# A two-layer encoder trunk on one core: first tiles and memory keys fetched a stage ahead, two units paired at a seam, roots and low parts moved

## What is computed

```python
def even_layer(x, mem, ...):              # layer 0
    h = rmsnorm(x, norm_g)
    qa, ka, va, ga, qb, kb, vb, gb, qm, gm = split_cols(h @ w_in, EVEN_SPLITS)
    oa = sliding_window_sink_attention(qa, ka, va, sinks)     # 8 heads
    ob = stick_breaking_attention(qb, kb, vb)                 # 8 heads
    om = memory_attention(qm, rmsnorm(mem, mem_norm_g), w_mem_kv)   # 4 heads, 256 memory tokens
    y = concatenate([oa * silu(ga), ob * silu(gb), om * silu(gm)])
    return x + y @ w_out                                      # y: 1280 columns

def odd_layer(x, mem, ...):               # layer 1
    h = rmsnorm(x, norm_g)
    qc, ckv, qi, ki, wi, gc, qm, gm = split_cols(h @ w_in, ODD_SPLITS)
    ckv = rmsnorm(ckv, kv_norm_g)
    oc = dsa_sparse_attention(qc, ckv, w_uk, w_uv, qi, ki, wi)  # 16 heads; each token keeps 256 keys
    om = memory_attention(qm, rmsnorm(mem, mem_norm_g), w_mem_kv)
    y = concatenate([oc * silu(gc), om * silu(gm)])
    return x + y @ w_out

result = rmsnorm(odd_layer(even_layer(x)), final_norm)
```

## Time and profile before

| | |
|---|---|
| Median of 3 executions | 3892.38 us (3891.35 to 3898.17) |
| The profiled execution, its own time | 3890.18 us |
| Its span in the trace | 3888.4 us |
| Granted TensorE clock, mean | 0.969 |
| PE busy | 3576.3 us, 92% |
| DVE / ACT / POOL busy | 2306.2 / 2064.0 / 773.7 us (59 / 53 / 20%) |
| DMA | 441.65 MB, mean 114 GB/s |

### The profile page before, as it was taken

How to read it: one execution, slowest core, us unless ns; L and a number is a source line. 1 busy time by engine, 2 the same in 40 slices (tenths; PEclk the granted TensorE clock), 3 DMA queues, 4 the chain that set the end, 5 groups by cost and what they waited for, 6 DMA issues and landing times. The chain is left out here.

```text
span 3888.4 us, 83330 instructions
## 1 busy us (share of the span) xinstructions
PE 3576.3 (92%) x32524; PEld 3085.4 (79%) x32524; DVE 2306.2 (59%) x5832; ACT 2064.0 (53%) x4636; POOL 773.7 (20%) x657
## 2 busy tenths in 40 slices
PE   5999999989899989979779989977899999999899
PEld 4777899978687768867557987966788888888687
DVE  6100110067899973320799989968677777777422
ACT  5222211156888862212677657554677777777311
...
GB/s 190 113 119 108 129 67 60 45 220 158 99 99 71 74 80 129 143 198 101 88 44 125 114 163 132 107 131 217 167 100 99 89 100 87 87 92 46 150 123 80
DMA packets 336462, 441.65 MB, mean 114 GB/s; under 512 B 18248, under 2 KB 255432, under 8 KB 326728
## 3 DMA queue, kind: packets, MB, share of 16 engines
...
...
## 5 line engine op out<-in xcount | busy, mean ns | idle before, releaser
L1296 PEld LDWEIGHTS s_o<-s_v,s_pT 128*64 128x64 f32 x13056 | 402.0, 138 | 90.0 <-issue 70.3
L1296 PE MATMUL s_o<-s_v,s_pT 128*64 128x64 f32 x13056 | 437.1, 224 | 20.4 <-issue 20.3
L215 PE MATMUL s_acc<-s_wh,s_hT 128*128 128x256 f32 (+1 forms) x1408 | 429.9, 305 | 7.2 <-ACT s_parts L628 3.1
L216 PE MATMUL s_acc<-s_wl,s_hT 128*128 128x256 f32 (+1 forms) x1408 | 429.2, 305 | 0.0
L217 PE MATMUL s_acc<-s_wh,s_hT 128*128 128x256 f32 (+1 forms) x1408 | 428.7, 305 | 0.0
L1449 ACT ACTIVATE s_probs<-s_probs,s_nmx 128x512 f32<-128x512 f32 (+3 forms) x640 | 417.0, 658 | 10.9 <-DVE s_nmx L1495 10.9
L1281 PE MATMUL s_s<-s_kh,s_qs 128*128 128x512 f32 (+3 forms) x944 | 378.0, 403 | 38.6 <-DMA s_qs<-fm 17.1
L215 PE MATMUL s_acc<-s_hT,s_wh 128*128 128x512 f32 x880 | 351.3, 399 | 63.0 <-DVE s_wl L314 25.8
L1484 DVE CUSTOM_DVE_ANT_0 s_probs<-s_s,s_scores 128x512 f32<-128x512 f32 (+3 forms) x640 | 371.4, 607 | 8.2 <-PEq L91 6.8
L2239 DVE TENSOR_SCALAR_CACHE_REDUCE s_scratch<-s_scores,s_thr 128x384 uint8<-128x384 f32 (+4 forms) x320 | 365.3, 1209 | 1.1
L216 PE MATMUL s_acc<-s_hT,s_wh 128*128 128x512 f32 x880 | 348.4, 396 | 0.0
...
## 6 DMA issues: line engine op xcount, KB each, us to landing
fm<-s_parts ACTq DMA_DIRECT2D x120, 512.0 KB, 2.8
s_qs<-fm SPq DMA_DIRECT2D x58, 512.0 KB, 6.3
y<-s_g SPq DMA_DIRECT2D x20, 1024.0 KB, 5.2
...
kc<-s_parts SPq DMA_DIRECT2D x32, 512.0 KB, 3.0
s_kh<-kc SPq DMA_DIRECT2D x30, 512.0 KB, 10.3
s_kl<-kc SPq DMA_DIRECT2D x30, 512.0 KB, 12.0
s_w<-in_o_fm SPq DMA_DIRECT2D x25, 512.0 KB, 4.6
```

The costliest lines, as they stand in the source:

```text
L215: nc.tensor.matmul(out, sh, mh, start=(j == 0), stop=False)
L216: nc.tensor.matmul(out, sh, ml, start=False, stop=False)
L1296: last = nc.tensor.matmul(o_ps[r:r + HD, 0:HD], pT[:, x * P + r:x * P + r + HD], v[:, g.u.kbs[g.a + x], vc:vc + HD], start=(g.first and x ...
```

## The change

Five things are changed.

1. **FirstTiles**, new: y of tile 0 and weight tiles 0 and 1 of each output projection get tiles and semaphores of their own, allocated before `stick_breaking` and `sparse_attention`. Those load the two weight tiles before the last pair's store. The last pair's store is made in four quarters (four blocks of tokens, 256 KB each); after the second, SP waits for the first quarter and loads y of tile 0. `out_project` starts at weight tile 2 and uses w0, w1, h2 and xn0 as its raw buffers; y of tile 1 follows weight tile 3.
2. **FirstKeys**, new: the memory keys of layer 1 (4 DMAs of 256 KB) are loaded in `latent_products`, behind the last rows of `ckv`; `short_attention` starts with q. The key buffers of `latent_products` go from 6 to 5 for the space.
3. **project_halves**: the first two units of the second half (16, 17) take turns: unit 16 tokens 0 to 511, unit 17 the same, then both for tokens 512 to 1023.
4. **latent_products**: on ACT the four roots of the second half of `ckv` stand six events later; on DVE four means stand together, ahead of the four reciprocals and normalizes; two groups of low parts stand inside `choose_two`, after its two scans, and no longer behind it.
5. `FirstHead` of layer 0 is allocated on the other side of SBUF, and three Scopes more are closed (two for FirstTiles, one for FirstKeys).

```diff
+    def events():
+        for u in range(NU):
+            if u == per:
+                for x in range(ng):
+                    yield u, x
+                    yield u + 1, x
+            elif u != per + 1:
+                for x in range(nt if unit(u)[2] else ng):
+                    yield u, x
+
+    def all_of(u):
+        return first_event(u + 1) + (u == per) * (ng - 1)
+
...
                     if u >= 2:
-                        pool.wait_ge(summed, first_event(u - 1))
+                        pool.wait_ge(summed, all_of(u - 2))
...
+                for e, (u, x) in enumerate(events()):
                     half, n, of_rows = unit(u)
-                    k, w, e0 = u % 2, width(u), first_event(u)
...
-    TG, NR = 2, 6
+    TG, NR = 2, 5
...
                 for q in range(4, NP):
                     load_rows(q)
+                keys.load(sp)
                 for f in range(NF):
                     send_columns(f)
...
                     squares(q)
-                    root(q)
                 for g in range(1, CH):
-                    evacuate(g * per, g * per + per // 2)
+                    evacuate(g * per, g * per + per // 4)
+                    if g == 1:
+                        for q in range(4, NP):
+                            root(q)
+                    evacuate(g * per + per // 4, g * per + per // 2)
...
+
+                    def low_parts():
+                        for t in range(4 + 4 * k, 8 + 4 * k):
+                            low_part(t)
+
+                    search.choose_two(dve, n, even, rank, low_parts if k in (1, 2) else None)
                     if k == 0:
                         for q in range(4, NP):
                             mean(q)
+                        for q in range(4, NP):
                             normalize(q)
-                    if k in (1, 2):
-                        for t in range(4 + 4 * k, 8 + 4 * k):
-                            low_part(t)
 
             @block.gpsimd
...
+class FirstKeys:
+    def __init__(self, nc, sc, k):
+        self.k = k
+        self.kh = sc.sb("kh", [P, PIECE], F32R, side="right")
+        self.kl = sc.sb("kl", [P, PIECE], F32R, side="right")
+        self.keys_in = sc.sem("keys_in")
+
+    def load(self, sp):
+        for half in range(2):
+            rows = slice(half * HD, half * HD + HD)
+            for to, rd in ((self.kh, self.k[0]), (self.kl, self.k[1])):
+                sp.dma_start(to[rows, :].bitcast(F32).rearrange("d (x k) -> d x k", x=M_HEADS),
+                             rd.rearrange("(x d) k -> d x k", x=M_HEADS)).then_inc(self.keys_in, 16)
...
-    def __init__(self, nc, sc, q_rows, k_rows, vals, gates):
+    def __init__(self, nc, sc, q_rows, k_rows, vals, gates, side=None):
         self.q_rows, self.k_rows, self.vals, self.gates = q_rows, k_rows, vals, gates
-        self.qs = sc.sb("qs", [P, S], F32R)
...
-                    sp.wait_ge(out_made, (p + 1) * 2 * NT)
-                    sp.dma_start(token_view(y_dram, A_HEADS * HD + p * P, P), gt[p % 2][:]
-                                 ).then_inc(y_stored[p % 2], 16)
+                    if p + 1 < PAIRS:
+                        sp.wait_ge(out_made, (p + 1) * 2 * NT)
+                        sp.dma_start(token_view(y_dram, A_HEADS * HD + p * P, P), gt[p % 2][:]
+                                     ).then_inc(y_stored[p % 2], 16)
+                tiles.load_weights(sp)
+                p = PAIRS - 1
+                for r in range(4):
+                    own = slice(r * NT // 4, (r + 1) * NT // 4)
+                    sp.wait_ge(out_made, (2 * p + 1) * NT + own.stop)
+                    sp.dma_start(token_view(y_dram, A_HEADS * HD + p * P, P)[:, own, :], gt[p % 2][:, own, :]
+                                 ).then_inc(last_stored if r else first_stored, 16)
+                    if r == 1:
+                        sp.wait_ge(first_stored, 16)
+                        tiles.load_rows(sp)
                 for k in range(2):
-                    sp.wait_ge(y_stored[k], 16 * (PAIRS // 2))
+                    sp.wait_ge(y_stored[k], 16 * len(range(k, PAIRS - 1, 2)))
+                sp.wait_ge(last_stored, 48)
 
             @block.tensor
...
-        kh = [sc.sb(f"kh{k}", [P, S], F32R) for k in range(NB)]
-        kl = [sc.sb(f"kl{k}", [P, S], F32R) for k in range(NB)]
+        kh = [keys.kh] if keys else [sc.sb(f"kh{k}", [P, S], F32R) for k in range(NB)]
+        kl = [keys.kl] if keys else [sc.sb(f"kl{k}", [P, S], F32R) for k in range(NB)]
...
-                                elif a == 0:
+                                elif a == 0 and not keys:
...
-                            pe.wait_ge(part_in[si][a], 96 if d.window or a == 0 else 32)
+                            pe.wait_ge(part_in[si][a], 96 if d.window or a == 0 and not keys else 32)
+                    if keys and p == 0:
+                        pe.wait_ge(keys.keys_in, 64)
...
-    def choose_two(self, dve, n, even, rank):
-        for one, other in zip(self.steps(n, even[0], rank[0]), self.steps(n + 1, even[1], rank[1])):
+    def choose_two(self, dve, n, even, rank, midway=None):
+        pairs = zip(self.steps(n, even[0], rank[0]), self.steps(n + 1, even[1], rank[1]))
+        for k, (one, other) in enumerate(pairs):
+            if midway and k == 2:
+                midway()
             dve.wait_ge(self.ch, self.links - 1)
             one().then_inc(self.ch, 1)
...
+class FirstTiles:
+    def __init__(self, nc, sc, y_dram, w_out, side=None):
+        self.y_dram, self.w_out = y_dram, w_out
+        self.y = sc.sb("y0", [P, YW], F32, side)
+        self.w = [sc.sb(f"w{j}", [P, D], F32, side) for j in range(2)]
+        self.y_in = sc.sem("y_in0")
+        self.w_in = sc.sems("w_in", 2)
+
+    def load_weights(self, sp):
+        for j in range(2):
+            sp.dma_start(self.w[j][:], self.w_out[j * P:(j + 1) * P, :]).then_inc(self.w_in[j], 16)
+
+    def load_rows(self, sp):
+        sp.dma_start(self.y[:], self.y_dram[0:P, :]).then_inc(self.y_in, 16)
...
-def out_project(nc, c, y_dram, w_out, resid, gain, h_dst=None, early=None, late_dram=None, out=None):
+def out_project(nc, c, y_dram, w_out, resid, gain, ahead, h_dst=None, early=None, late_dram=None, out=None):
...
-        y = [sc.sb(f"y{k}", [P, YW]) for k in range(2)]
-        h = [sc.sb(f"h{k}", [P, D]) for k in range(3)]
+        y = [ahead.y, sc.sb("y1", [P, YW])]
+        h = [*ahead.w, sc.sb("h2", [P, D])]
...
-                load_y(0)
-                for j in range(KY):
+                for j in range(2, KY):
                     if j >= len(raw):
                         sp.wait_ge(w_split, j - len(raw) + 1)
                     sp.dma_start(raw[j % len(raw)][:], w_out[j * P:(j + 1) * P, :]).then_inc(w_in[j], 16)
-                    if j == 1:
+                    if j == 3:
                         load_y(1)
...
-                              [fm0[n, k0:k0 + HD, :] for n in range(2)], vb, gb)
+                              [fm0[n, k0:k0 + HD, :] for n in range(2)], vb, gb, side="right")
             short_attention(nc, c, [window_heads(fm0, va, ga, y0, 0), window_heads(fm0, va, ga, y0, 1),
                                     memory_heads(fm0, km0, vm0, gm0, y0, (A_HEADS + B_HEADS) * HD)], ahead)
-            stick_breaking(nc, c, fm0, vb, gb, y0, ahead)
+            first = Scope(nc)
+            tiles = FirstTiles(nc, first, y0, a["e_w_out"][0])
+            stick_breaking(nc, c, fm0, vb, gb, y0, ahead, tiles)
...
-        out_project(nc, c, y0, a["e_w_out"][0], x, a["o_norm"], h_dst=h1, early=hT, late_dram=late_dram)
+        out_project(nc, c, y0, a["e_w_out"][0], x, a["o_norm"], tiles, h_dst=h1, early=hT, late_dram=late_dram)
+        first.close()
...
                 early.close()
+                held = Scope(nc)
+                keys = FirstKeys(nc, held, [km1[n] for n in range(2)])
                 latent_products(nc, c, ckv, a["o_kv_norm"], a["o_uk"], a["o_w_uv"][0].rearrange("l h d -> l (h d)"),
-                                kc, vc, search)
+                                kc, vc, search, keys)
...
-            short_attention(nc, c, [memory_heads(fm1, km1, vm1, gm1, y1, C_HEADS * HD)], ahead)
-            sparse_attention(nc, c, fm1, kc, vc, gc, y1, scores, ahead)
-        out_project(nc, c, y1, a["o_w_out"][0], h1, a["final_norm"].rearrange("(a n) -> a n", a=1), out=out[0])
+            short_attention(nc, c, [memory_heads(fm1, km1, vm1, gm1, y1, C_HEADS * HD)], ahead, keys)
+            held.close()
+            first = Scope(nc)
+            tiles = FirstTiles(nc, first, y1, a["o_w_out"][0], side="right")
+            sparse_attention(nc, c, fm1, kc, vc, gc, y1, scores, ahead, tiles)
+        out_project(nc, c, y1, a["o_w_out"][0], h1, a["final_norm"].rearrange("(a n) -> a n", a=1), tiles, out=out[0])
+        first.close()
 
```

151 lines of the change are left out of this document (82 added, 69 removed).

## The result

| | before | changed |
|---|---|---|
| Median, first chip | 3892.34 us (3891.35 to 3898.17, 4 executions) | 3857.55 us (3853.0 to 3871.24, 4 executions) |
| Ratio, first chip | | 0.9918, 95% interval 0.9902 to 0.9935 |
| Ratio, the same kernel again, two other sessions | | 0.9918 (0.9905 to 0.9931), 0.9908 (0.9893 to 0.9923) |
| The profiled execution, span | 3888.4 us | 3869.5 us |

What follows compares the result with a forecast made beforehand. PE, busy 92% of the span, was taken to bound most stages, with gains only where it stands still; the terms summed to -22.5 us, from the profiled 3890.18 to 3867.7, median 3869.9 predicted, range 3862 to 3879.

Steps and rivals of the forecast that it cites:

- the landing of the last quarter: End of both attentions: the last 256 KB store lands in 3.1 us, where 1 MB takes 5.0.
- the length of the rounds of weight tiles: Output projections: from the split of tile 1 to the last split, two rounds still take 13.7 us.
- last store in quarters: End of stick-breaking and sparse attention: a 256 KB store replaces 1 MB behind the last block, -1.9 us a seam.
- first tiles: Start of both output projections: y of tile 0 and two weight tiles already there, -3.8 us a seam.
- paired units: Seam of the halves: unit 17's first event runs in PE's wait for `hT`, -5.5 us.
- latent products: DVE's waits for roots and squares go but for one hand-over, and the last key store leaves earlier: -2.3 us.
- memory attention: Start of layer 1's memory attention: the second half of q is issued and lands earlier, -4.5 us.
- three closings: Three more Scope closings between stages, 0.4 us each: +1.2 us.
- Rival D: Ends of both attentions: each quarter store lands in 5.0 us like the whole; -18.7 us, 3873.7, chance 0.10.
- Rival A: Several seams: landings bound, DMAs set the weight rounds, smaller gain of -15.6 us, 3876.8; chance 0.22.
- Rival C: Seam of the halves: ACT waits for DVE, PE misses half an event per remaining bit; +14 us, 3906, chance 0.03.
- the tail behind DVE: End of latent products: the stage ends with DVE and not the last key store's landing, -0.7 us.

Runs made afterwards that it cites:

- the repeat: The changed kernel run again unaltered: ratio to the kernel before 0.9918, profiled span 3856.2 us.
- experiment 7: The changed kernel with the last pair's store whole again and y of tile 0 not loaded ahead, weight tiles still ahead: ratio to before 0.9958.
- experiment 10: The changed kernel with weight tiles 0 and 1 of the output projections split ahead of y of tile 0: ratio to before 0.9915.
- Kernels 4 and 1: 4: the changed kernel with the old project_halves, paired units undone, ratio to before 0.9936; 1: the changed kernel again, unaltered, 0.9918.
- Experiment 9: The changed kernel with ACT's budget of counts one event earlier in the second half: ratio to before 0.9934.
- experiment 8: The kernel before with ACT's budget of counts one event later in the second half: ratio to before 1.0043.
- experiment 5: The changed kernel with the two groups of low parts back behind choose_two, roots and means left as changed: ratio to before 0.9912.

## Why the prediction was wrong

The direction, the places and the hiding were right; the sum was a third too small, and it failed at four terms: the landing of the last quarter, the length of the rounds of weight tiles, a second gain of the pair and a second gain in the latent products. No one of them alone explains it. The bounds of the terms, added up, give -33.7 and not the -33 of the prediction; the measured gain lies about there, since four terms fell the same way. Term by term, in us:

| term | predicted | measured |
|---|---|---|
| last store in quarters, two seams | -3.8 | -5.6 (6.16 to 3.40, 6.33 to 3.51) |
| first tiles, two seams | -7.6 | -10.3 by the last split; -9.3 by the two stages |
| paired units | -5.5 | -10 by the stage, -7 to -9 by the ratios |
| latent products | -2.3 | -5, start of the search taken apart (search and what is behind it: 107.2 in the mean of 4 profiles without the change there, 102.0 with it) |
| memory attention | -4.5 | -4.3 (the stage's mean of 4 profiles without and 10 with it, 76.9 to 73.0, less a closing) |
| three closings | +1.2 | +1.1 |
| sum | -22.5 | -30 to -34 by the terms, -32 to -36 by the times of the kernels |

**The quarter.** The step that failed took the landing of 256 KB from a store of `vc`, 3.1 us, and called it a lone one. It was not alone: 0.4 us ahead of it SP had issued a store of `kc` of 512 KB. The last quarter is alone and lands in 2.3. The Trainium skill, "DMA: Bandwidth & Descriptors", section "Anatomy of one DMA — SWDGE (gpsimd) path", puts 2.0 us fixed and bytes over 436 GB/s, for DMAs issued by GpSimd, where these are issued by SP; that would be an estimated 2.6, 3.2 and 4.4 us for the three sizes (not the 2.75 that the prediction worked out for the first), where 2.3, 3.2 and 5.0 were measured. Rival D, that small stores land no faster, is out.

**First tiles.** The prediction followed the right chain and mis-sized two of its terms. It kept the two rounds at 13.7 us, and it put the split of tile 1 at 6.6. In the repeat tile 1 is split at 6.3 and the rounds take 5.9 and 6.6 us in place of 6.9 and 6.8: the first is a us shorter, since tile 5 lands 3.5 us after its issue where it took 4.5. In the first profile's first seam it is the other term: tile 1 is split at 5.3 and the rounds take 13.5. Over both seams that is some 3 us more than the forecast. That it lands faster because less is queued ahead of it (1.7 MB fewer in all) is borne out by experiment 7, where it took 3.6 us with the DMA engines mostly idle, and its first round 5.9; experiment 10 shows that an earlier issue doesn't help further. Rival A named the stream of loads as the limit, but drew from it a smaller gain.

**The pair.** The step that was missing is the second term, 4.6 us or more at the units 24 to 26. ACT may empty banks only after the counts that its budget puts before them; a count waits for a threshold of DVE; GpSimd works off ACT's banks before it splits the next weights. DVE's 16 us at the seam left it late against a budget that goes by events, and that lateness reached PE some 90 us later. Rival C named ACT waiting for thresholds and had the wrong sign: the pair shortens DVE's stall, so PE misses less, not more. Kernels 4 and 1, which differ in the pair alone, show each link: DVE's thresholds 9.4 us late behind the seam and 3.2 at unit 24, ACT's waits 25.5 us in place of 11.5, GpSimd's splits 3 us late. Experiment 9 shows that the budget reaches PE; experiment 8 that PE's waits also depend on where in an event ACT's waits fall, which no run takes apart. The path of rival C itself, PE waiting for a bank, did occur, but in experiment 8 (5.0 us).

**The latents.** DVE's waits went as predicted (1.9 and none left, where I kept 0.3). Two things were priced at nothing or too low: with PE and GpSimd ten us earlier, the last steps of the search have no GpSimd beside them (L2353 for two rows 6.48 us, now 4.35), and the tail behind DVE, put at 0.7 us of gain, which in two of the five profiles with GpSimd as late as before was 5.1 us and not 1.8. What decides between 1.8 and 5.1 is whether GpSimd ends behind DVE, as in experiment 5.

**The memory attention and the closings** came as worked out: PE's first product at 5.0 to 5.8 us in place of 10.4 to 10.7. The store of the memory attention and the next load, one closing more between them:

```profile
2764.80 0.36 SPq L1938 DMA_DIRECT2D y<-s_g  x1
2770.38 0.48 SPq L1399 DMA_DIRECT2D s_qs<-fm  x1
```

5.58 us in place of 5.20: 0.38 for a closing, 0.4 predicted.

Not tried: five key buffers for six, and FirstKeys by itself. With five buffers ACT waits once for a key store, 0.4 to 1.0 us in three profiles, where with six it never did; the prediction had no such wait.
